# First block of a two-block layer stack: order of x's products, masks, heads' sums, up projections and the LRU recurrence

## The reference, cut to what matters

```python
proj = rmsnorm(h, norm1_g) @ w_in                      # 1024 -> 6144 columns
q_pre, f_pre, i_pre, og_pre, lx, ly, ga, gb = split(proj)
o_a = hgrn2_branch(q_pre, f_pre, i_pre, og_pre, ...)   # gated linear attention, 4 heads of 128
o_b = rglru_branch(lx, ly, ...)                        # conv of width 4, LRU recurrence over time
merged = sigmoid(ga) * (o_a @ w_up_a) + sigmoid(gb) * (o_b @ w_up_b)
h = h + merged @ w_out
h = h + hier_moe(rmsnorm(h, norm2_g), ...)             # 32 experts, top 1 group, top 2 experts in it
h = rmsnorm(h, final_g)
```

## Time and profile before

| | us |
|---|---|
| three runs | 1207.93, 1209.44, 1210.05; median 1209.44 |
| the profiled execution's own time | 1208.81 |
| its span, from the first to the last instruction | 1206.9 |
| TensorE busy in the span | 1029.2 |
| up_a starts | 200.40 |
| up_b starts, output projection starts | 215.17, 242.88 |
| the experts' loads follow each other without a gap from | 285.08 |
| the first load of the second block has landed | 711.2 |

### The profile page before, as it was taken

The page is one execution under the profiler, slowest core; times in us unless marked ns, Lnnn a source line. Parts: engine busy times, 40 slices in busy tenths (PEclk is TensorE's granted clock), DMA queues, the critical chain, the costliest instruction groups (busy, mean ns, idle before and its releaser), DMA issues.

```text
span 1206.9 us, 14776 instructions
## 1 busy us (share of the span) xinstructions
PE 1029.2 (85%) x6310; PEld 680.3 (56%) x6310; DVE 511.6 (42%) x893; ACT 219.0 (18%) x453; POOL 17.1 (1%) x53
## 2 busy tenths in 40 slices
PE   8999999999666565647474689999999999999997
PEld 4999988855221212222222234444688859999743
DVE  6659745663110101010100048655465666656644
ACT  2535355011000000000000022222323102111101
POOL 1000000000000000000000010000000000000000
PEclk9999999999887878787888899999999999999999
DMA  9542337889999999999999995555332426554400
GB/s 341 210 153 80 130 140 283 280 324 394 429 426 431 427 426 430 427 427 428 428 428 425 416 388 213 198 196 189 140 140 70 140 70 227 169 181 143 172 1 35
DMA packets 88396, 318.49 MB, mean 264 GB/s; under 512 B 8836, under 2 KB 34552, under 8 KB 77576
## 3 DMA queue, kind: packets, MB, share of 16 engines
q1 hardware_dynamic: 80416, 314.58, 66.4%
q10 hardware_dynamic: 7912, 2.92, 1.0%
HBM read 316.44 MB, written 1.05 MB: 263 GB/s over the span
## 4 chain that ended last, share of the span: by engine, by line
PE 64%; DMA 29%; DVE 4%; ACT 1%; issue 1%; SPq 1%; POOL 0%; POOLq 0%; DVEq 0%; ACTq 0%
DMA arena<-in_w_up 27%; PE bank L1457 11%; PE bank L847 10%; PE bank L1328 9%; PE bank L1540 5%; PE bank L1113 5%; PE bank L1302 5%; PE bank L1042 4%; PE bank L1424 2%; PE bank L1020 2%; DMA ring<-in_w_in 2%; PE bank L826 1%; PE bank L923 1%; PE bank L1010 1%; PE bank L1104 1%
## 5 line engine op out<-in xcount | busy, mean ns | idle before, releaser
L1113 PE MATMUL bank<-arena 128*32 128x512 f32 x336 | 126.3, 729 | 49.9 <-DMA arena<-in_w_up 49.9
L1113 PE MATMUL bank<-ring,arena 128*32 128x512 f32 x448 | 126.3, 728 | 0.0
L2538 DVE TENSOR_TENSOR h<-h,bank 128x512 f32<-128x512 f32 x8 | 5.5, 686 | 268.2 <-PE bank L1113 255.8
L1113 PE MATMUL bank<-extra,arena 128*32 128x512 f32 x112 | 62.8, 726 | 64.2 <-DMA arena<-in_w_gate 64.2
L1151 PE MATMUL bank<-arena 128*32 128x512 f32 x224 | 60.3, 700 | 38.2 <-DMA arena<-in_w_down 37.7
L1328 PE MATMUL bank<-ring,arena 128*128 128x512 f32 x200 | 87.1, 593 | 0.0
L1113 PEld LDWEIGHTS bank<-arena 128*32 128x32 f32 x336 | 31.7, 132 | 95.2 <-issue 95.2
L1457 PE MATMUL bank<-arena,ring 128*128 128x128 f32 x704 | 82.4, 275 | 0.0
L1457 PEld LDWEIGHTS bank<-arena,ring 128*128 128x128 f32 x704 | 80.5, 192 | 0.5 <-DVE arena L2066 0.2
L1113 PEld LDWEIGHTS bank<-extra,arena 128*32 128x32 f32 x112 | 14.0, 131 | 109.2 <-issue 109.2
L1328 PEld LDWEIGHTS bank<-ring,arena 128*128 128x128 f32 x200 | 37.7, 190 | 45.5 <-issue 45.4
(11 more groups left out here) (435 smaller groups left out, 1686.2 us busy)
## 6 DMA issues: line engine op xcount, KB each, us to landing
ring<-in_w_in SPq DMA_DIRECT2D x26, 2048.0 KB, 14.3
ring<-in_w_gate SPq DMA_DIRECT2D x16, 2048.0 KB, 40.0
arena<-in_w_up SPq DMA_DIRECT2D x16, 2048.0 KB, 35.4
ring<-in_w_up SPq DMA_DIRECT2D x16, 2048.0 KB, 40.0
ring<-in_w_down SPq DMA_DIRECT2D x16, 2048.0 KB, 39.5
arena<-in_w_down SPq DMA_DIRECT2D x15, 2048.0 KB, 35.3
extra<-in_w_gate SPq DMA_DIRECT2D x8, 2048.0 KB, 34.4
arena<-in_w_gate SPq DMA_DIRECT2D x8, 2048.0 KB, 47.6
```

The costliest lines, as they stand in the source:

```text
L1113: last = mm(bank[b][e * CAP:(e + 1) * CAP, :], main.xgT[:, k, e * CAP:(e + 1) * CAP], w[e][:, k, :], start=(k == 0), stop=(k == KC - 1))
```

## The change

- `turn_x` can be called for one half. The right half of x's tile 0 is turned between the steps k = 1 and k = 2 of the first product and no longer ahead of k = 0.
- The masks of levels 3 and 4 and those of levels 5 and 6 (with the final value of mask 7) move from unit 1 to two places in unit 0.
- `heads_sums` goes ahead of half5(9). `head_roots` is split: the Ln stand between hold_first1(9) and hold_fifth1(9), the Exp after it, and `lru_sigmoids(0)` comes right behind the Exp and ahead of the evacuation of block D.
- The up_a columns are computed in the order 2, 6, 3, 7, 1, 5, 0, 4. The wait for the held fifth product (bank 5) stands before column 1, that for block C (bank 4) before column 0.
- `lru_exps` increments `decay` after its Exp and again after its Tanh. The combination, the square root, the product, the scans and the last product are done for blocks 0 to 3 and then for 4 to 7; `ob_ready` counts to 2.
- up_b is computed in two parts, first the steps of up_b0 for all eight columns, then those of up_b1. The slot of up_b0 is free after the first part (`half_projected`).

```diff
-        return ("projected_a", 1) if name == "up_a" else ("projected_b", KC)
+        return {"up_a": ("projected_a", 1), "up_b0": ("half_projected", 1), "up_b1": ("projected_b", KC)}[name]
...
-                    sp.wait_ge(S("ob_ready"), 1)
+                    sp.wait_ge(S("ob_ready"), 2)
...
-            def turn_x(t):
-                for half in range(2):
+            def turn_x(t, halves=(0, 1)):
+                for half in halves:
...
-            turn_x(0)
+            turn_x(0, (0,))
...
+                    if t == 0 and k == 2:
+                        turn_x(0, (1,))
                     if t == 0 and k == 4:
                         turn_x(1)
                         take1(0)
...
                     half1(v + 1)
+                    if v == 8:
+                        heads_sums()
                     if v == 9:
                         lru_pair(5)
                     half5(v + 1)
-                    if v == 8:
-                        heads_sums()
...
-            pe.wait_ge(S("held"), 2 * NH)
-            pe.wait_ge(S("unit_out"), evacuated(NH - 1, "C"))
             pe.wait_ge(S("oa_ready"), 1)
             take1(13)
-            for m in range(KC):
+            for m in (2, 6, 3, 7, 1, 5, 0, 4):
+                if m == 1:
+                    pe.wait_ge(S("held"), 2 * NH)
+                if m == 0:
+                    pe.wait_ge(S("unit_out"), evacuated(NH - 1, "C"))
...
             unit_out(pe, NH - 1)
-            pe.wait_ge(S("ob_ready"), 1)
-            up_b = [take1(14), take1(15)]
-            for m in range(KC):
-                if m >= 4:
-                    pe.wait_ge(S("merged"), m - 3)
-                for k in range(KC):
-                    last = mm(columns(0, m), w3(up_b[k // 4], 4)[:, k % 4, m * P:(m + 1) * P],
-                              ly[:, k, :], start=(k == 0), stop=(k == KC - 1))
-                last.then_inc(S("projected_b"), 1)
+            for part in range(2):
+                s = take1(14 + part)
+                pe.wait_ge(S("ob_ready"), part + 1)
+                for m in range(KC):
+                    if part and m >= 4:
+                        pe.wait_ge(S("merged"), m - 3)
+                    for k in range(4):
+                        last = mm(columns(0, m), w3(s, 4)[:, k, m * P:(m + 1) * P], ly[:, 4 * part + k, :],
+                                  start=(part == 0 and k == 0 and m < 4), stop=(part == 1 and k == 3),
+                                  skip_group_check=True)
+                    if part:
+                        last.then_inc(S("projected_b"), 1)
+                if part == 0:
+                    last.then_inc(S("half_projected"), 1)
...
-            def head_roots():
+            def head_logs():
...
+            def head_exps():
+
                 act.wait_ge(S("root"), 2)
                 A_(rsn, rsn, ACT.Exp, scale=-0.5).then_inc(S("root"), 1)
...
                     last = A_(lrua[:, b, :], lrur[:, b, :], ACT.Exp, scale=m2sp[:, b:b + 1])
+                last.then_inc(S("decay"), 1)
...
                     hold_first1(v + 1)
+                    if v == 8:
+                        head_logs()
                     if v == 9:
                         lru_sigmoids(5)
                     hold_fifth1(v + 1)
...
                 elif v == 8:
-                    head_roots()
+                    head_exps()
+                    lru_sigmoids(0)
                 elif v == 9:
                     lru_sigmoids(6)
                 unit_evac(v, "D")
...
-            act.wait_ge(S("root_args"), 1)
-            A_(lrut, lrut, ACT.Sqrt).then_inc(S("root"), 1)
+            for c in range(2):
+                act.wait_ge(S("root_args"), c + 1)
+                A_(lrut[:, 4 * c:4 * c + 4, :], lrut[:, 4 * c:4 * c + 4, :], ACT.Sqrt).then_inc(S("root"), 1)
...
                 sum_unit(u, 4)
-                if u == 1:
+                if u == 0:
+                    level_masks(range(3, 5))
+                elif u == 1:
                     forget_sums()
...
-                if u == 1:
-                    level_masks(range(3, 7))
+                if u == 0:
+                    level_masks(range(5, 7))
...
+            dve.wait_ge(S("decay"), 10)
             for c in range(2):
-                last = v.scalar_tensor_tensor(out=lrut[:, 4 * c:4 * c + 4, :], in0=lrut[:, 4 * c:4 * c + 4, :],
-                                              scalar=1.0, in1=lrur[:, 4 * c:4 * c + 4, :], op0=ALU.add, op1=ALU.mult)
-            last.then_inc(S("root_args"), 1)
-            dve.wait_ge(S("root"), 4)
-            link(v.tensor_tensor(lrui, lrui, lrut, ALU.mult))
-            for c in range(KC):
-                last = v.tensor_tensor_scan(lrut[:, c, :], lrua[:, c, :], lrui[:, c, :], 0.0, ALU.mult, ALU.add)
-            link(last)
+                half = slice(4 * c, 4 * c + 4)
+                v.scalar_tensor_tensor(out=lrut[:, half, :], in0=lrut[:, half, :], scalar=1.0, in1=lrur[:, half, :],
+                                       op0=ALU.add, op1=ALU.mult).then_inc(S("root_args"), 1)
             unit_out(dve, 5)
-            v.tensor_tensor(ly, ly, lrut[:, :, META:TT], ALU.mult).then_inc(S("ob_ready"), 1)
+            for c in range(2):
+                half = slice(4 * c, 4 * c + 4)
+                dve.wait_ge(S("root"), 4 + c)
+                link(v.tensor_tensor(lrui[:, half, :], lrui[:, half, :], lrut[:, half, :], ALU.mult))
+                for k in range(4 * c, 4 * c + 4):
+                    last = v.tensor_tensor_scan(lrut[:, k, :], lrua[:, k, :], lrui[:, k, :], 0.0, ALU.mult, ALU.add)
+                link(last)
+                v.tensor_tensor(ly[:, half, :], ly[:, half, :], lrut[:, half, META:TT], ALU.mult).then_inc(S("ob_ready"), 1)
```

More of the change, by code:

```diff
@@ L1770, in _ @@
                     copy_state()
-                elif v in (8, 9):
-                    lru_sigmoids((0, 7)[v - 8])
+                elif v == 9:
+                    lru_sigmoids(7)
                 unit_evac(v, "C")
@@ L2402, in sum_out_weights @@
                     v.tensor_tensor(b21, b21, ts[2], ALU.subtract).then_inc(S("out_summed"), 1)
-            dve.wait_ge(S("ob_ready"), 1)
+            dve.wait_ge(S("ob_ready"), 2)
             for step in range(3):
```

## The result

The changed kernel takes 1204.49 us (median of 8 runs, 1203.45 to 1207.18) against 1209.70 us for the kernel before in the same comparison (8 runs, 1207.93 to 1211.08): ratio 0.9955, 95% interval 0.9943 to 0.9967. The forecast was 1203.8 us.

What follows compares the result with a forecast made beforehand. Expert-weight DMA bounds 297 to 711 us; TensorE's earlier program sets when the full stream starts. Gains 0.89 + 0.61 + 1.32 + 2.80 = 5.62 us off the profiled 1208.81 give 1203.2, forecast 1203.8 us as median, range 1201.8 to 1207.0.

Steps and rivals of the forecast that it cites:

- The frame: TensorE's waits in the first block move unit 12's load at 285.08 us, and stream and end follow one for one.
- Rivals 3: Expert-weight stream: its end is fixed by its bytes alone, so the gain is hidden, 1209.4 us; chance 0.05.
- 4: Stream from 285 us: its rate suffers from the first loads' new order and spacing; 1212.3 us at 2%; chance 0.05.
- wait 1: TensorE waiting for the second half of x's first tile, until 7.38 us; removing it gains 0.89 us.
- 14.04 - 13.15: Start of the first product's last four products, old minus new, in us: a gain of 0.89 us.
- lands 9.8 us later, at 13.05: The 1 MB load issued at 3.25 us lands then; the first product's last four products need it.
- Wait 2: half5(3) at 61.07 us, held by VectorE's mask operations ahead of a weight sum; moving them gains 0.61 us.
- Wait 3: Second lru pair at 167.00 us, held by ScalarE's chain to the first sigmoid; reordering the heads' work gains 1.32 us.
- rival 2: ScalarE's three table loads still end after 167 us, so another wait replaces the heads' one; 1205.1 us; chance 0.10.
- Waits 4 and 5: TensorE before up_a (200.40 us) and up_b (215.17 us); column order and halves gain 2.80 us together.
- 1.9 (only wait 4 goes): Lower end for the up projections' pair: 1.9 us gained if only the wait before up_a disappears.
- rival 1: The clock falls in the new wait at 12 to 13 us: 1.5 us less gain, 1205.3 us; chance 0.17.

Runs made afterwards that it cites:

- run 3: The changed kernel with all columns of up_a computed a second time (64 instructions more): 1217.6 us, ratio 1.0062 to the kernel before.
- run 8: The changed kernel with every later round's token gather done twice, inside the full stream: 1204.51 us, ratio 0.9956 to the kernel before.
- run 1: The kernel before with only the new order of up_a's columns and its two later waits: 1211.8 us, ratio 1.0011 to the kernel before.
- run 2: The kernel before with only the recurrence and up_b done in halves: 1208.61 us, ratio 0.9991 to the kernel before.
- run 6: The changed kernel with both halves of x's first tile turned ahead of the first product again: 1206.24 us, ratio 0.9968 to the kernel before.
- run 5: The changed kernel again, unchanged, on the second chip: 1203.98 us, ratio 0.996 to the kernel before.
- run 9: The changed kernel with the heads' edits alone undone (heads' sums, root steps, first sigmoids as before): 1206.25 us, ratio 0.9973 to the kernel before.
- run 11: The changed kernel once more, unchanged, beside runs 10 and 12: 1204.0 us, ratio 0.9956 to the kernel before.
- run 4: The changed kernel with the first unit's 1 MB load issued as two 512 KB loads, products beginning on the first: 1204.22 us, ratio 0.9953 to the kernel before.
- run 12: Run 4's kernel again (the changed kernel with the 1 MB load in two): 1204.12 us, ratio 0.995 to the kernel before.
- run 7: Run 4's kernel with two unneeded 128x512 products in TensorE's wait for the router: 1202.49 us, ratio 0.9945 to the kernel before.
- run 10: Run 7's kernel again (split load and two extra products in the router's wait): 1202.65 us, ratio 0.9945 to the kernel before.

## Why the prediction was right

**The frame.** The time follows unit 12's load one for one: 5.21 us earlier at the issue, 5.36 at the end, at the same 428 GB/s. Runs 3 and 8 show both sides of that border. Rivals 3 and 4 fall. That the sum came within 0.3 us (5.62 forecast, 5.36 in the profiles, 5.21 in the medians) is in part luck: wait 1 brought 0.53 us less than forecast, and 0.24 us that nothing in the forecast stands for came in behind up_b.

**Wait 1, mis-sized: 0.36 instead of 0.89 us.** The order of events was as forecast (products at 6.46, transposes, products, wait, the landing); the term 14.04 - 13.15 was too large at both ends. 14.04 is a row of the chain of waits, which begins where the row before it ends by the modelled end. The timeline has the start of these instructions in the kernel before:

```profile
13.87 3.60 PE L826 MATMUL bank<-ring,arena 128*128 128x512 f32 x8
```

That is 0.17 us of the missing 0.53. The step "lands 9.8 us later, at 13.05" took the landing as a constant: here the 1 MB load took 10.1 us, landed at 13.35, and the products began at 13.41 instead of 13.15, another 0.26. The last 0.10 is that the eight instructions took 3.70 us behind the wait instead of 3.60. Over the ten traces with the load whole, the load took 9.4 to 10.6 us. By the starts of the eight instructions behind it, the old order (before and runs 1, 2 and 6) has 13.87, 13.85, 13.15 and 13.43, mean 13.58 us; the new one with the load whole (after and runs 3, 5, 8, 9 and 11) 13.41, 12.67, 13.35, 13.86, 13.93 and 13.36, mean 13.43. That is 0.15 us, less than the scatter, and one of the six paid 1.7 us by the clock. So in the traces the edit's direct worth is about nothing; the lower end given was -0.6. The run times speak for more: run 6's median is 2.3 us above the changed kernel's. Whether that comes from where the later clock fall lands, as its one trace suggests for 1.4 us, is open.

**Wait 2, right.** 0.72 against 0.61 us; the extra 0.1 is what TensorE loses in its first instructions after a wait (16 of them took 2.12 us before and 2.02 now), which I had not counted. The masks' cover held in both places.

**Wait 3, right: 1.19 against 1.32 us.** Shifted by the 1.08 us already won, ScalarE's chain is the one worked out, to within 0.1 us a step: Ln from 159.33 (159.3), the copy's end 161.49 (161.5), the Exp's 163.87 (163.85), the load's 165.17 (165.1), the pair from 165.81 (165.75). The 0.24 us of wait left is under the 0.5 forecast. The 0.07 us that I gave back for "the old pair took 0.07 longer" did not come: the new pair takes 1.16 too. Run 9 gives the same 1.19 by taking the edit out. The Trainium skill (ScalarE: Activation LUTs, What ACT_TABLE_LOAD costs) adds a drain to each switch; the trace does not agree, since the operation behind the sigmoid's load starts 0.01 us after the load's end (162.81 + 1.28, then 164.10). By the page's drain, as an estimate, the pair would have waited beyond 167 and rival 2 would have won; as it is, rival 2 falls.

**Waits 4 and 5, right: 2.85 against 2.80 us.** The lower end, "1.9 (only wait 4 goes)", named the wrong lower end: run 1 shows that the order of up_a alone gives 0 because the same recurrence ends wait 5, and run 2 that the halves alone give 0.9. The two edits are one. Both waits were covered by 4 and 13 us, as forecast (206.1 against 210.05, 211.2 against 223.9).

**The clock.** Of the six traces with the new wait the products behind it ran at full rate in five; rival 1, at 0.17, occurred in the sixth (run 9). Not foreseen was the fall around the router (next section), which decides 1.4 to 2.5 us of a run and which the forecast's scatter covered only by luck.

## What to carry to other kernels

Find the event that starts the bandwidth-bound stretch and count only what stands ahead of it; one experiment that adds work on each side of it settles the frame. Two waits in a row that hang on the same chain of another engine are one gain: removing the first alone only lengthens the second, so shorten the chain or price the pair together. Where a wait ends on a load's landing, take its scatter from several executions before counting tenths, and ask whether what is won before it merely hides something, as the early products hide a slow start here. When one wait is taken away, look which engine would be late next, as VectorE with its mask operations is in runs 4 and 12.

## What the hardware showed that was not expected

- **Clusters of times.** Runs of one kernel fall into groups some 3 us apart (run 2: 1206.9 to 1207.4 and 1209.8 to 1211.3). The traces show something that costs up to 2.5 us and may be the cause, though one to three traces for each kernel cannot show it: the granted clock falls to 0.50 for 3 to 6 us in the stretch of small products around the router. It falls beside VectorE's routing work, where it costs nothing (after, runs 3, 5, 8 and 11), ahead of the added products, where it costs 1.3 us (run 7, and run 10 has the same rows), on the gather (1.4 us in runs 1 and 6, 1.6 in run 9, 2.5 in run 2), or not at all (before, runs 4 and 12). What decides between these is not settled.
- **The same place, both ways.** The wait of 1.96 us before 13.41 left the clock at 1.00, that of 2.45 us before 13.93 in run 9 was followed by 0.68.
- **A record that isn't complete.** In runs 7, 8, 10 and 12 the first four product instructions took 3.38 to 3.74 us instead of 1.96, yet the window over them reads 1.00; the row below is run 12's. There a single 128x512 instruction took 1.05 to 1.19 us instead of 0.59, and a weight load 0.33 instead of 0.19. The same holds for the eight instructions in runs 2 and 6 (4.96 and 5.25 us at a recorded 1.00), which took about as long as the 5.19 us of the kernel before, where the record falls to 0.50. I read this as a fall that the record misses, so that the duration of one known instruction tells the level more surely.

```profile
6.60:10.00 3.40, 3.40 (x4) 1.36 (x5) 0.00 (x0) 1.81 (x2) 0.00 (x0) 1.00 1.04 383
```
